# First modulation of a decoder layer: summed in quarters on TensorE, inputs scaled by VectorE

## The reference

```python
cond = jax.nn.silu(c)
mod = cond @ w_ada[layer] + b_ada[layer]          # (1024) @ (1024, 6 * 1024)
shift1, scale1, gate1, shift2, scale2, gate2 = jnp.split(mod, N_MOD, axis=-1)
h = modulate(rms_norm(x), shift1, scale1)         # rms_norm(x) * (1 + scale1) + shift1
y = hybrid_mixer(h, layer, w_in[layer], ...)      # starts with h @ w_in
```

## Time and profile before

| | us |
|---|---|
| median of 3 executions | 1147.61 |
| lowest, highest | 1146.69, 1148.62 |
| the profiled execution's own time | 1148.47 |
| its span (what the rows count in) | 1146.7 |
| busy in the span: TensorE | 1126.4 (98%) |
| VectorE | 875.2 (76%) |
| ScalarE | 612.4 (53%) |
| GpSimd | 496.3 (43%) |

### The profile page before, as it was taken

How to read it: one execution, slowest core, us unless ns; L and a number is a source line. 1 busy time by engine, 2 the same in 40 slices (tenths; PEclk the granted TensorE clock), 3 DMA queues, 4 the chain that set the end, 5 groups by cost and what they waited for, 6 DMA issues and landing times.

```text
span 1146.7 us, 15528 instructions
## 1 busy us (share of the span) xinstructions
PE 1126.4 (98%) x5483; PEld 932.4 (81%) x5483; DVE 875.2 (76%) x1035; ACT 612.4 (53%) x933; POOL 496.3 (43%) x318
## 2 busy tenths in 40 slices
PE   7899999999999999999999999999999999999997
PEld 7788787888888888888888888888888888888786
DVE  6898987779788776379975675567795785966776
ACT  7763554766666675346555455545654433524425
POOL 1021023235354355347542434243576575765750
PEclk9999999999999999999999999999999999999998
DMA  9767477445363457613255533554425537438203
GB/s 357 270 228 257 159 182 217 99 127 157 100 185 94 145 183 219 203 55 127 102 168 175 184 129 124 170 184 161 151 74 190 186 101 268 154 129 284 65 2 147
DMA packets 162948, 186.71 MB, mean 163 GB/s; under 512 B 7604, under 2 KB 119352, under 8 KB 159928
## 3 DMA queue, kind: packets, MB, share of 16 engines
q1 hardware_dynamic: 160472, 179.44, 46.9%
q0 software_dynamic: 2400, 6.29, 2.8%
HBM read 138.51 MB, written 40.89 MB: 156 GB/s over the span
## 4 chain that ended last, share of the span: by engine, by line
PE 92%; DVE 2%; DMA 1%; issue 1%; ACT 1%; SPq 1%; POOL 0%; DVEq 0%; ACTq 0%
PE unit_bank L1807 19%; PE unit_bank L2260 9%; PE unit_bank L2262 9%; PE unit_bank L2261 9%; PE small_bank L2261 9%; PE small_bank L2262 9%; PE small_bank L2260 9%; PE small_bank L1807 4%; PE unit_bank L2095 4%; PE unit_bank L2097 3%; PE unit_bank L2096 3%; PE small_bank L1846 1%; DVE ada_acc L2361 1%; DMA ada_slot<-in_w_ada_dram 1%; PE small_bank L1949 1%
## 5 line engine op out<-in xcount | busy, mean ns | idle before, releaser
L1039 POOL TENSOR_TENSOR wr_lo<-quarter,wr_hi 128x512 fp32r<-128x512 f32 x122 | 196.6, 1625 | 173.9 <-ACT wr_hi L1596 173.9
L2260 PE MATMUL unit_bank<-op_hi,wr_hi 128*128 128x512 f32 x452 | 176.7, 391 | 0.9 <-issue 0.9
L2262 PE MATMUL unit_bank<-op_hi,wr_lo 128*128 128x512 f32 x452 | 175.9, 389 | 0.0
L2261 PE MATMUL unit_bank<-op_lo,wr_hi 128*128 128x512 f32 x452 | 175.8, 389 | 0.0
L2260 PE MATMUL small_bank<-op_hi,wr_hi 128*128 128x512 f32 x448 | 174.5, 390 | 0.0
L2261 PE MATMUL small_bank<-op_lo,wr_hi 128*128 128x512 f32 x448 | 174.3, 389 | 0.0
L2262 PE MATMUL small_bank<-op_hi,wr_lo 128*128 128x512 f32 x448 | 174.3, 389 | 0.0
L1596 ACT ACTIVATE wr_hi<-wr_full 128x512 fp32r<-128x512 f32 x90 | 56.8, 631 | 177.4 <-DVE wr_full L3044 171.0
L3044 DVE TENSOR_TENSOR wr_full<-quarter,quarter 128x512 f32<-128x512 f32 x90 | 89.1, 991 | 57.8 <-PE small_bank L2262 23.0
L1596 ACT ACTIVATE wr_hi<-quarter 128x512 fp32r<-128x512 f32 x136 | 82.7, 625 | 86.6 <-PE unit_bank L2262 47.3
L1807 PE MATMUL unit_bank<-a_hi,w_hi 128*128 128x512 f32 x304 | 121.1, 398 | 0.0
(11 more groups left out here) (387 smaller groups left out, 2372.8 us busy)
## 6 DMA issues: line engine op xcount, KB each, us to landing
quarter<-in_w_mlp_dram SPq DMA_DIRECT2D x128, 256.0 KB, 4.1
hidden_scratch<-hid SPq DMA_DIRECT2D x98, 256.0 KB, 2.4
ada_slot<-in_w_ada_dram SPq DMA_DIRECT2D x48, 512.0 KB, 6.9
op_full<-hidden_scratch SPq DMA_DIRECT2D x21, 1024.0 KB, 4.9
pair_quarter<-in_w_in_dram SPq DMA_DIRECT2D x32, 256.0 KB, 3.2
piece_x<-t_scratch SPq DMA_DIRECT2D x16, 512.0 KB, 4.6
piece_y<-t_scratch SPq DMA_DIRECT2D x32, 256.0 KB, 3.4
raw<-in_w_out_dram SPq DMA_DIRECT2D x16, 512.0 KB, 4.8
```

The source lines that it names most:

```text
L1039: pool.tensor_tensor(wr_lo[slot][:, :, :], split_source(n), wr_hi[slot][:, :, :].bitcast(F32), ALU.subtract).then_inc(wr_lo_pool, 1)
L2260: pe.matmul(dst, wh, ah, start=opens, stop=False, skip_group_check=True)
L2261: pe.matmul(dst, wh, al, start=False, stop=False, skip_group_check=True)
L2262: mm = pe.matmul(dst, wl, ah, start=False, stop=k == KH - 1, skip_group_check=True)
```

## The change

The work of the opening is cut in quarters of 256 features (two tiles k) instead of halves, and the sums move between engines.

- Pieces 0 to 15 are cut anew: piece n holds depth tiles 2k and 2k + 1 (k = n % 4) of quarter n // 4, for shift and scale, and is loaded by two DMAs of 256 KB.
- Of each quarter's four pieces VectorE sums `BY_VECTOR` of them as before (0, 2, 2, 1 for quarters 0 to 3). The others TensorE multiplies straight from the landing slots: eight one-column products of a piece with `cond`, which sum over depth tiles and partitions at once; four closing products add VectorE's sums.
- Tiles are no longer scaled by a product with a diagonal. One product of `ones` with four tiles' diagonals puts the token scales of 512 tokens on all partitions (`token_scales`, once for each half), and VectorE makes a scaled input from `xT`, scale 1 and these (`scaled_input`). The shift comes in rounding: ScalarE's `high_input` adds it as a bias, VectorE's `low_input` adds it and subtracts the high part in one instruction.
- Units 0 and 1 are loaded behind the fourth token tile, then pieces 0 to 3, then token tiles 4 to 7, then the rest. Piece 8 and later wait for the quarter that held their slot to be finished.
- The four squares of token tiles 4 to 7 move on ScalarE behind the first two high parts, each ahead of its tile's copies; ScalarE makes all copies of these tiles.
- TensorE's main records go in the order of quarters and halves: quarter 0 half 0, quarter 0 half 1, quarter 1 half 0, quarter 1 half 1, then the rest.

The squares stand behind the weights' and the inputs' high parts and alternate with copies. The diff, cut to its core:

```diff
+BY_VECTOR = (0, 2, 2, 1)
...
-            return (g, q % 8, q // 8) if g == 0 else (g, q // 2, q % 2)
+            return (g, q % 4, q // 4) if g == 0 else (g, q // 2, q % 2)
+
+        def input_number(k, half):
+
+            return 4 * (k // 2) + 2 * half + k % 2 + 1
+
+        INPUTS = [(k, half) for q in range(4) for half in range(2) for k in (2 * q, 2 * q + 1)]
+        QUARTER_BANK = (UB[3], SB[0], SB[1], SB[0])
...
-                    sp.wait_ge(ada_added, last[0] + 1)
+                    sp.wait_ge(ada_added, 4 * (last[0] // 4) + 4 if last[0] < 16 else last[0] + 1)
                 if n == 37:
                     sp.wait_ge(filled["z"], 4)
                 g, k, h = ada_piece(n)
                 if g == 0:
-                    src = w_ada[0, k * P:(k + 1) * P, 0:2 * D].rearrange("p (a n) -> p a n", a=2)
-                    sp.dma_start(ada_slots[slot][:, :].rearrange("p (a n) -> p a n", a=2),
-                                 src[:, :, h * (D // 2):(h + 1) * (D // 2)]).then_inc(ada_loaded[slot], 16)
+                    src = w_ada[0, 2 * k * P:2 * (k + 1) * P, 0:2 * D].rearrange("(kk p) (a n) -> p kk a n", p=P, a=2)
+                    for kk in range(2):
+                        sp.dma_start(ada_slots[slot][:, kk * HALF:(kk + 1) * HALF].rearrange("p (a n) -> p a n", a=2),
+                                     src[:, kk, :, h * 2 * P:(h + 1) * 2 * P]).then_inc(ada_loaded[slot], 8 * 2)
...
-            for t in range(3, TT):
+            load_x(3)
+            load_unit(0, 0, w_in, 0, GLR)
+            load_unit(1, 1, w_in, 0, GK)
+            for n in range(4):
+                load_ada(n)
+            for t in range(4, TT):
                 load_x(t)
             sp.wait_ge(consts, 12)
             for p in range(0, P, 32):
                 sp.dma_start(w2_full[p:p + RANK, :], gate_w2[0]).then_inc(w2_loaded, 16)
-            for n in range(8):
+            for n in range(4, 16):
                 load_ada(n)
-            load_unit(0, 0, w_in, 0, GLR)
-            load_unit(1, 1, w_in, 0, GK)
-            for n in range(8, 20):
+            load_unit(2, 0, w_in, 0, GQ)
...
+            def high_input(k, half):
+
+                act.wait_ge(normalised, input_number(k, half))
+                act.wait_ge(ada_added, 4 * (k // 2) + 4)
+                act.activation(tok(a_hi[:, k], half), tok(a_full[:, k], half), ACT.Identity, bias=col(mod, k), scale=1.0
+                               ).then_inc(split_hi, 1)
...
-            act.wait_ge(read["x"], 2 * (TT - 3))
-            copy_x(TT - 3)
-            for n in range(11):
-                if n in (4, 7):
-                    copy_x(TT - 2 if n == 4 else TT - 1)
-                copy_scaled(n)
-                if n == 9:
-                    for u in range(2):
-                        high_of(u)
...
+            roots(0)
+            for u in range(2):
+                high_of(u)
+            for k, half in INPUTS[0:2]:
+                high_input(k, half)
+            act.wait_ge(read["x"], 8)
+            for t in range(4, TT):
+                square_x(t)
+                copy_x(t)
+            roots(1)
+            for k, half in INPUTS[2:]:
+                high_input(k, half)
+                if (k, half) == (5, 0):
+                    high_of(2)
...
-            def first_ada(q, b):
-
-                pe.wait_ge(ada_added, 8 * (q // 2 + 1))
-                for j in range(4):
-                    mm = product(SB[b][:, j:j + 1], ada_acc[:, (4 * q + j) * P:(4 * q + j + 1) * P], ones[:, 0:1])
+            def first_ada(q):
+
+                dst, mine = QUARTER_BANK[q], range(BY_VECTOR[q], 4)
+                if q == 0:
+                    pe.wait_ge(setup, 5)
+                elif q < 3:
+                    pe.wait_ge(read["x"], 2 * TT - 2 + q)
+                else:
+                    pe.wait_ge(read["ada"], 2)
+                for kp in mine:
+                    wait_ada(pe, 4 * q + kp)
+                    for kk in range(2):
+                        for j in range(4):
+                            at_ = (4 * kk + j) * P
+                            mm = pe.matmul(dst[:, j:j + 1], ada_slots[ADA_SLOT[4 * q + kp]][:, at_:at_ + P],
+                                           cond[:, 2 * kp + kk:2 * kp + kk + 1], start=(kp, kk, j) == (mine[0], 0, 0),
+                                           stop=(kp, kk) == (3, 1) and not BY_VECTOR[q], skip_group_check=True)
+                if BY_VECTOR[q]:
+                    pe.wait_ge(modulated, sum(n > 0 for n in BY_VECTOR[:q + 1]))
+                    for j in range(4):
+                        mm = pe.matmul(dst[:, j:j + 1], ada_acc[:, (4 * q + j) * P:(4 * q + j + 1) * P], ones[:, 0:1],
+                                       start=False, stop=True, skip_group_check=True)
...
-            for t in range(TT - 3):
+            for t in range(4):
...
-            for n in range(2 * TT):
-                j, t = divmod(n, TT)
-                if n in (0, 4):
-                    pe.wait_ge(diag_ready, n // 4 + 1)
-                if n in (2, 4, 7):
-                    turn_x({2: TT - 3, 4: TT - 2, 7: TT - 1}[n])
-                if n == 11:
+            def token_scales(half):
+
+                pe.wait_ge(diag_ready, half + 1)
+                if half == 0:
                     pe.wait_ge(read["rows"], 1)
-                    for q in range(2):
-                        first_ada(q, 2 + q)
-                if n >= 4:
-                    pe.wait_ge(normalised, n - 3)
-                for i in range(4):
-                    mm = product(UB[NORM_BANK[n]][:, i * P:(i + 1) * P],
-                                 x_stage[t][:, (4 * j + i) * P:(4 * j + i + 1) * P], t1[:, t * P:(t + 1) * P])
-                mm.then_inc(scaled_x, 1)
-
-            for k4 in range(2):
+                product(SB[2 + half][:, :], ones[:, :], tok(t1, half)).then_inc(scaled_x, TT)
+
+            def first_units(q, half):
+
+                for k in (2 * q, 2 * q + 1):
+                    for u in range(2):
+                        half_unit(u, u, half, a_hi, a_lo, split_ready(0), (k,))
+
+            token_scales(0)
+            first_ada(0)
+            first_units(0, 0)
+            for t in range(4, TT):
+                turn_x(t)
+            token_scales(1)
+            first_ada(1)
+            first_units(0, 1)
+            first_units(1, 0)
+            first_ada(2)
+            first_units(1, 1)
+            first_ada(3)
+            for q in (2, 3):
                 for half in range(2):
-                    if k4 == 0:
-                        pe.wait_ge(normalised, 2 * TT - 2 + 2 * half)
-                    for k in range(4 * k4, 4 * k4 + 4):
-                        for u in range(2):
-                            half_unit(u, u, half, a_hi, a_lo, split_ready(0), (k,))
-                        if (k, half) == (0, 1):
-                            pe.wait_ge(read["x"], 16)
-                            for q in range(2, 4):
-                                first_ada(q, q - 2)
+                    first_units(q, half)
...
+            def finish_first(q):
+
+                dve.wait_ge(filled["ada"], q + 1)
+                for i, (one_more, sem_, by) in enumerate(((0.0, ada_added, 4), (1.0, read["ada"], 1))):
+                    at_ = 8 * i + 2 * q
+                    dve.scalar_tensor_tensor(mod[:, at_:at_ + 2], QUARTER_BANK[q][:, 2 * i:2 * i + 2], one_more,
+                                             cols[:, at_:at_ + 2], ALU.add, ALU.add).then_inc(sem_, by)
...
-            for n in range(16):
-                add_ada(n)
-                if n == 0:
-                    diagonals(1)
-                if n == 8:
-                    finish_ada(0, 0, 2)
-                    finish_ada(0, 1, 3)
-                if n == 9:
-                    pack_gate()
-                    low_weights_first(1)
-                if 10 <= n < 15:
-                    low_input(n - 10)
-            for i in range(5, 7):
-                low_input(i)
-            finish_ada(0, 2, 0)
...
+            def scaled_input(k, half):
+
+                dve.wait_ge(scaled_x, TT * (half + 1))
+                dve.wait_ge(read["x"], TT * (half + 1))
+                dve.wait_ge(read["ada"], k // 2 + 1)
+                dve.scalar_tensor_tensor(tok(a_full[:, k], half), tok(xT[:, k], half), col(mod, 8 + k), SB[2 + half][:, :],
+                                         ALU.mult, ALU.mult).then_inc(normalised, 1)
+
+            def low_input(k, half):
+
+                dve.wait_ge(split_hi, input_number(k, half))
+                dve.wait_ge(ada_added, 4 * (k // 2) + 4)
+                dve.scalar_tensor_tensor(tok(a_lo[:, k], half), tok(a_full[:, k], half), col(mod, k),
+                                         tok(a_hi[:, k], half).bitcast(F32), ALU.add, ALU.subtract).then_inc(lo_dve, 1)
+
+            def first_inputs(q, half):
+                for k in (2 * q, 2 * q + 1):
+                    scaled_input(k, half)
+                for k in (2 * q, 2 * q + 1):
```

(41 more changed lines are left out.)

88 lines of the change are left out of this document (18 added, 70 removed).

## The result

The changed kernel takes 1179.58 us in the median (1179.01 to 1181.64); the kernel before, run beside it, 1147.8 (1146.69 to 1148.62). The ratio is 1.0279, interval 1.0266 to 1.0292: 2.8% slower. The profiled execution took 1179.01, its span is 1177.3, against 1148.47 and 1146.7 of before.

A forecast was written before the change was run, and what follows sets the result against it. TensorE was taken to bound the kernel, with the opening's delay passed on nearly whole. The walk's +12.0 us (6.3 of it added work) and +4.4 for a low clock gave +16.4, a median of 1164.0 us, range 1156 to 1182.

The forecast's parts named there:

- likeliest case: Whole kernel: the walk plus a clock that falls in two pauses, +16.4 us, median 1164.0 us; chance 0.40.
- Bound, and the opening alone: TensorE, busy 98% of the span, bounds the kernel; a shift of the opening's end passes on nearly whole.
- end mark: Start of the first product behind the first two units, ending the opening: 58.58 us before, 69.8 walked.
- Price of a pass with the clock up: TensorE's opening: each pass costs 0.11 us, with one column or 128, because the weight load is paid.
- faster rival: The four bursts: one-column passes cost less in long bursts; at half price 1149.8 us, at 0.025 1145; chance 0.03.
- The walk: The opening's four engines carried forward in order at trace prices: +11.2 us at its end, +12.0 in all.
- +0.8: Behind the opening: the gate's second low part is ready at about 73.5 where TensorE wants it at 72.8.
- +4.4: Second token product and quarter 1's burst: low clock behind TensorE's two pauses, +4.4 us beyond the walk.
- second rival: The four bursts: one-column bursts don't hold the clock, +24 us over the walk, 1184 us; chance 0.20.
- +3.5: Quarter 1's burst: 40 passes at 0.20 for 0.11 us under a low clock, +3.5 us.
- +0.9: Second token product: run under a low clock behind TensorE's pauses, +0.9 us.
- case without a fall: Whole opening: the clock never falls, so only the walk's +12.0 us counts, 1159.6 us; chance 0.28.

The follow-up runs named there:

- e1: The changed kernel with 128 equal columns in place of one in every product of the four bursts; 1164.44 us, ratio 1.0133.
- e2: The changed kernel with ScalarE's squares of token tiles 4 to 7 and the second roots moved ahead of its first high parts; 1172.29 us, ratio 1.0202.
- e3: The kernel before, with its first burst of one-column small sums issued four times over (64 passes for 16); 1154.51 us, ratio 1.0053.
- e8: The changed kernel, one-column bursts kept, with pauses filled: two tiles' transposes ahead of the first main records, some squares, low parts and loads earlier; 1165.04 us, ratio 1.0148.
- e4: The kernel before, with its first burst of small sums issued four times over and 128 columns in each product; 1151.04 us, ratio 1.0024.
- e7: The changed kernel with 128-column bursts, pauses filled by reordering, and VectorE summing two pieces of every quarter; 1153.4 us, ratio 1.0051.
- e9: e7 with unit 2's load and high part moved earlier, so that GpSimd's subtraction for it falls elsewhere; 1151.93 us, ratio 1.0032.

## Why the prediction was right in sign and range, and wrong in its likeliest case

**Bound, and the opening alone: right.** +31.2 us at the end mark gave +30.6 in the span, and no wait of over 1.1 us lies behind it. The chance of 0.94 for slower rested on the count of passes, and it held.

**Price of a pass with the clock up, 0.11: right.** Quarter 2's burst is 3.62 for 32 passes, e1's first 7.31 for 64. The faster rival (0.03 a pass) is gone: a one-column pass costs as much as one with 128 columns, in a long burst too, and no burst here came under 0.11.

**The walk: right but for one small term.** In e1 the first burst runs from 14.40 to 21.6, as walked; the first main record comes at 24.63 for 24.35. The end mark there is 73.29, of which the low clock is 3.4 (1.65 in the first ten main records, which take 3.95 for 2.3, 1.4 in quarter 1's burst, 0.3 in the token product): 69.9 without it, if all of it is passed on, for 69.8 walked. Scaled inputs cost 0.67 (0.62 taken, up to 1.0 allowed), and loads in rows of 1 KB kept up: no burst of the changed kernel waits for one. ScalarE's late squares held the second token product back as walked: in e2, which takes that away, it comes at 38.84 for 44.16, with no pause ahead. The +0.8 for the gate's second low part did not show: its product is at 92.75, 31.2 behind the 61.53 of before, like the first.

**The clock: the step that failed.** I put +4.4 for it, on the premise that it falls only in pauses, and put what a burst of one-column passes does to it at nothing, outside the second rival. Against the walk's 69.8 the end mark came at 89.81, +20.0, and e1 shows what part the columns have: 73.29 to 89.81 is 16.5. By the rows the excess lies in the bursts (quarter 0: 13.17 for 7.31 in e1; quarter 1: 6.38 and 1.84 for 3.73 and 1.05; quarter 3: 7.26 and 1.84 for 5.52 and 1.05; quarter 2 none: 11.8 us together) and in the main records behind them, 0.43 apart for 0.23, some 2 us in each of four groups (8.3 by the starts). The 1.8 us burst of the earlier trace rows had gone by without a fall, and the forecast carried that over to bursts of 4.4 to 7.1 us. e3 shows why it didn't carry: in the same place, with the burst made longer, the clock was still full from 30 to 31 and fell between 31 and 32, later than the 29.4 at which the burst of before had ended.

The +4.4 was not well put together for the pauses alone either. e1 has both pauses nearly as walked (2.92 and 2.63 us) and a fall behind each, but the clock was back before half of quarter 1's passes were done: +1.4 for my +3.5, and +0.3 for +0.9 in the token product. The low clock in the ten main records, which I took to be hidden since ScalarE would lead, costs its whole 1.65: ScalarE's first copy waits 3.82 us for TensorE's transposes, as my own walk had it. The sum of the three, 3.4, is near 4.4 by luck.

**The second rival: right, in mechanism and nearly in size.** It said that bursts of one column do not hold the clock, most of 200 passes at 0.20 (+13) and each group of main records behind one low (+2.1 each, and 3 elsewhere), +24 over the walk and 1184; measured are 11.8, 8.3, +20.0 and 1179.6. It is smaller by quarter 2's burst, which ran at 0.11, and by the 3 elsewhere. I gave it 0.20 where the forecast had 0.40 and the case without a fall 0.28. With no row for a burst over 1.8 us on either side, and 20 us between it and the forecast, the shares were not earned by the trace. The range held only because it reached to the rival's lower half; the time lies 2.4 us below its upper end and 15.6 above the forecast. The Trainium skill, "TensorE: Matmul & The Clock Gate", section "HAM oscillation — how this bites in real kernels", lays falls of the clock to pauses of TensorE. e1's two falls behind pauses agree; e3 and e8, with falls where TensorE had stood for no more than 0.93 and 0.34 us ahead of the burst, go beyond that rule.

**Pause and burst together.** A pause ahead does bear on a narrow burst: behind one the fall comes sooner. Read from stretches of 1 us, the clock fell 0.5 us behind the first pass of the changed kernel's bursts of quarters 0 and 1, ahead of which TensorE had stood for 1.8 and 2.6 us (1.2 and 1.0 us in quarter 0 of e2 and e8, with the same 1.8). Where it had stood for at most 0.93 us, the fall came 3.2 to 5.4 us behind the first pass: 4.8 and 3.2 in quarters 2 and 3 of the changed kernel, 3.3 and 4.1 in quarters 1 and 2 of e2, 5.4, 5.0 and 3.5 in quarters 1 to 3 of e8, 3.8 in e3. Quarter 1's burst has both: 0.5 us in the changed kernel, and 3.3 in e2, where the pause of 2.6 us ahead of it is filled. So quarter 2's burst, 4.4 us long with full work ahead, was over at 0.11 before the clock fell, and the main records behind it ran low, while quarter 1's ran low almost from its start.

**What stays open.** Why the fall comes after 3.2 us in one burst and after 5.4 in another is told by no run. How many columns are enough was not tried.

## What to carry to other kernels

Work moved to TensorE as one-column products costs its weight loads, 0.11 us a pass, and when the burst is long it can cost the clock as well, in the burst and for microseconds of full-width products behind it. If such a burst is longer than any that the profile shows, price it at both levels and let the range cover both; giving the products 128 equal columns costs next to nothing at full clock (the same weight loads; 32 passes take 3.73 us for 3.62) and took back 15 of the 32 us here. Of a busy engine with a low clock ask what it is busy with, and not only where it stood.

## What the runs showed of the hardware that I had not expected

- TensorE's granted clock fell from full to 0.50 while TensorE was 100% busy with one-column float32 passes (e3, 64 of them), and did not in 64 passes of 128 columns at the same place (e4).
- A pass has the same price with 1 and with 128 columns at full clock (0.11 us), and 0.20 us at half clock.
- A pause of 1.8 or 2.6 us ahead of a narrow burst went with a fall 0.5 to 1.2 us behind its first pass; where TensorE had stood for at most 0.93 us, it came after 3.2 to 5.4 us (changed kernel, e2, e3, e8).
- A VectorE sum of 512 columns with two SBUF inputs took 2.76 us for 0.75 beside a GpSimd subtraction of 2.34, and moving that subtraction by 16 us moved the stretch to another instruction (e7, e9). An instruction with one of its operands in PSUM was not stretched (e9).
